# A timetable of a streaming block: the scores' pieces of blocks 2, 3 and of blocks 6, 7 are given earlier ticks

## What is computed

```
h   = RMSNorm(x)
[q|k|v|xc|B|C] = h @ W_in                          # 1024 x 3072
sb  = StickBreaking(QKNorm(q), QKNorm(k), v)       # 8 heads x 64, strictly causal
cv  = B * causal_depthwise_conv3(C * xc)           # 512 channels
x   = x + concat(RMSNorm(sb), RMSNorm(cv)) @ W_out
h2  = RMSNorm(x)
q1, q2 = halves of (h2 @ peer_w_q) per head (8 heads, 2 x 128)
s1, s2 = q1 @ sub_keys[0].T, q2 @ sub_keys[1].T    # 128 scores each
idx, gate = top 16 of the sums of top 16 of s1 and top 16 of s2; softmax
y   = x + sum over 8 heads, 16 picks of gate * gelu(h2 . U[idx]) * V[idx]
```

## Time and profile before

| | before |
|---|---|
| median of 3 runs | 2874.86 us (2873.90 to 2875.57) |
| profiled execution | 2879.8 us, span 2878.0 us |
| TensorE (PE) busy | 2225.2 us, 77% |
| VectorE (DVE) busy | 1983.9 us, 69% |
| ScalarE (ACT) busy | 1093.7 us, 38% |
| GpSimd (POOL) busy | 1103.9 us, 38% |
| DMA | 1183.89 MB, mean 411 GB/s |
| of it the gathers (q0) | 147456 packets, 1073.81 MB, 90.5% of 16 engines' span |
| weights, x and out (q1) | 108.17 MB, 9.6% |

### The profile page before, as it was taken

The page is one execution under the profiler, slowest core; times in us unless marked ns, Lnnn a source line. Parts: engine busy times, 40 slices in busy tenths (PEclk is TensorE's granted clock), DMA queues, the critical chain, the costliest instruction groups (busy, mean ns, idle before and its releaser), DMA issues. The chain is left out here.

```text
span 2878.0 us, 29917 instructions
## 1 busy us (share of the span) xinstructions
PE 2225.2 (77%) x9210; PEld 1012.2 (35%) x9210; DVE 1983.9 (69%) x4782; ACT 1093.7 (38%) x3164; POOL 1103.9 (38%) x1037
## 2 busy tenths in 40 slices
PE   9788889778977887778986888777898656555555
PEld 6535525333532343333542244333354111111111
DVE  3757766787666668786767666888666666666654
ACT  2333432552333335562333334666233322322222
POOL 0333433343343334443344333444334444434442
PEclk9999999989998998899998999999999776777787
DMA  9999999999999999999999999999999999999998
GB/s 390 359 413 403 398 419 418 419 412 412 385 421 420 419 419 412 419 415 416 412 420 420 418 410 416 410 417 415 419 405 420 416 422 419 421 418 416 415 421 353
DMA packets 178865, 1183.89 MB, mean 411 GB/s; under 512 B 19856, under 2 KB 21520, under 8 KB 47632
## 3 DMA queue, kind: packets, MB, share of 16 engines
q0 software_dynamic: 147456, 1073.81, 90.5%
q1 hardware_dynamic: 31248, 108.17, 9.6%
HBM read 1177.70 MB, written 4.19 MB: 411 GB/s over the span
## 5 line engine op out<-in xcount | busy, mean ns | idle before, releaser
L1472 DVE CUSTOM_DVE_ANT_0 ring<-ring,h2r 128x1024 f32<-128x1024 f32 x1024 | 1249.0, 1223 | 781.2 <-DMA ring<-table_uv,idx_t 772.1
L643 POOL DMA_INDIRECT ring<-table_uv,idx_t x1024 | 1102.0, 1076 | 1755.0 <-DVE dots L1472 1128.9
L911 PE MATMUL acc<-ring,wmask 128*64 128x512 f32 x4096 | 1200.6, 715 | 578.2 <-ACT wmask L1069 574.2
L911 PEld LDWEIGHTS acc<-ring,wmask 128*64 128x64 f32 x4096 | 283.4, 153 | 1286.4 <-ACT wmask L1069 845.9
L1064 ACT ACTIVATE dots<-dots 128x2 f32<-128x2 f32 x512 | 104.1, 203 | 1530.5 <-DVE dots L1472 1528.0
L1069 ACT ACTIVATE wmask<-gmask,dots 128x64 f32<-128x64 f32 x1024 | 300.3, 340 | 48.6 <-ACT dots L1064 1.5
L1057 ACT ACTIVATE gmask<-stack,gate_t 128x64 f32<-128x64 f32 x1024 | 293.1, 334 | 0.6 <-DVE gate_t L1459 0.5
L666 PE MATMUL pt<-hT,w_held 128*128 128x256 f32 (+1 forms) x560 | 109.3, 344 | 0.0
L666 PEld LDWEIGHTS pt<-hT,w_held 128*128 128x128 f32 x560 | 88.2, 193 | 28.2 <-issue 21.1
L1064 ACT ACT_TABLE_LOAD x73 | 93.7, 1283 | 1.3
L657 PE MATMUL pz<-w_ring,hT 128*128 128x512 f32 x192 | 90.8, 615 | 0.0
(11 more groups left out here) (274 smaller groups left out, 2171.6 us busy)
## 6 DMA issues: line engine op xcount, KB each, us to landing
w_ring<-wstream SPq DMA_DIRECT2D x121, 512.0 KB
ring<-wstream SPq DMA_DIRECT2D x32, 512.0 KB, 11.7
ring<-table_uv,idx_t POOLq DMA_INDIRECT x1024
w_held<-wstream SPq DMA_DIRECT2D x11, 512.0 KB, 13.4
xs<-x_in_dram SPq DMA_DIRECT2D x8, 512.0 KB
h2r<-wstream SPq DMA_DIRECT2D x8, 512.0 KB, 14.8
scores<-wstream SPq DMA_DIRECT2D x8, 512.0 KB, 15.4
xs<-wstream SPq DMA_DIRECT2D x4, 512.0 KB, 12.3
```

What stands on the lines that cost most here:

```text
L643: nc.gpsimd.indirect_dma_start(out=ring[:, cell(t):cell(t) + 2, :].rearrange("p c d -> p (c d)"), out_offset=None, in_=table, in_offset=ba ...
L911: mm = nc.tensor.matmul(acc[HALF * i:HALF * i + HALF, half * 512:(half + 1) * 512], wmask[:, slot, :], ring[:, cell(2 * p + i) + 1, half * ...
L1472: V.tensor_tensor_reduce(u, u, h2r[:, b % H_SLOTS, i, :], 1.0, 0.0, ALU.mult, ALU.add, dots[:, t % SLOTS:t % SLOTS + 1]).then_inc(dots_don ...
```

## The change

Two numbers of `WHEN` change: the middle tick of blocks 2 and 3 from 224 to 217, that of blocks 6 and 7 from 732 to 727. Start and end ticks stay.

```
 REST_BEGIN = 3
-WHEN = [(-1, -1, 16), (8, 66, 84), (72, 224, 262), (262, 470, 514), (521, 732, 775)]
+WHEN = [(-1, -1, 16), (8, 66, 84), (72, 217, 262), (262, 470, 514), (521, 727, 775)]
 RANK_TIME = [0, 2, 4, 7, 9, 11, 14, 15, 17, 20, 25]
```

## The result

| | before | after |
|---|---|---|
| median | 2874.86 us | 2883.30 us |
| lowest to highest of 7 runs each | 2872.92 to 2878.27 | 2880.47 to 2886.05 |
| profiled execution | 2879.8 us (span 2878.0) | 2883.3 us (span 2881.5) |

The ratio is 1.0025, with a 95% interval of 1.0015 to 1.0036, so 4.3 to 10.3 us more. A second series of the same two kernels, beside the experiments, gave 1.0017 (1.0008 to 1.0026). I had forecast 2871.9 us, with a range that ended at 2878.5.

The account below looks back on a forecast made before the run. The DMA gathers were taken as the bound, so a new order could only win or lose time short of gathers. Terms -3.5 + 0 + 0.5 + 0 = -3.0 us gave 2871.9 us, range 2865.5 to 2878.5.

Parts of the forecast that it names:

- Term (1): Blocks 2 and 3: scores six ticks ahead of the rank remove VectorE's 9.5 us wait; -3.5 us, bounds 0 and -6.4.
- Both estimates behind the 3.5: For the rank's wait: gather at 757.47 us delayed by 3.2 us; hole differences to other blocks, 3.5 and 4.9 us.
- rival A: At block 2's rank: TensorE's mixes held the gathers anyway, 0.5 us won and lost again; 2874.9 us, chance 0.15.
- Term (2): TensorE's rush in both block pairs moves seven and five ticks sooner, same contents, not eased; 0, bounds 5.8 won, 2 lost.
- Term (3): Steps before the middle ticks, 5% and 2.3% closer among the sticks; 0.5 us lost, bounds 1 won, 5.7 lost.
- The sign that I had set for trouble: Over either stretch of sticks, a rate under 410 GB/s would show the forecast wrong; 412 to 415 was expected.
- Term (4): 65 pick steps of blocks 1, 4 and 5 move by -3 to +4 ticks; 0, half a microsecond either way.
- Rival C: Closer sticks saturate VectorE, 9.1 us more lost there; slower by 5.6 us, up to 2882.5 us; chance 0.08.
- Rival B: Both holes at TensorE's rush close, backlog from late dots or full clock; 9.3 us won, 2865.6 us; chance 0.17.
- what I worked out beside it from the Trainium skill's page: Denser steps release the clock throttle, so blocks 2 and 3's rush starts at full clock; -5.8 instead of -3.0 us.

## Why the prediction was wrong, point by point

**Term (1), -3.5 us for the rank's wait: the first step that failed.** The wait went, as foretold, and was worth 0 (-2.3 to +2.6). Both estimates behind the 3.5 were unsound. The issue of one gather 3.2 us late was a true delay, though its row names a mix as releaser, and it went with the wait (1.24 us behind the one ahead, for 4.4), but the whole stretch from gather 216 to 230 is only 0.3 us shorter; a delay counts only if the gathers around it don't take it up. And 6.4 - 2.9 us compared one trace's hole with another place's, when the same program gave a hole of 4.5 us in place of 6.3 (ticks 208 to 230) in another execution. On this term rival A, at 0.15, was right; its time, 2874.9, was not.

**Term (2), the rush "with the same contents": the step that set the sign.** Its own pieces and mixes are the same. But I looked at what moves and not at what it moves past. `turn_picks(1,3)` keeps tick 215 and the look-ups beside it stay at 206 to 211; before, they stood ahead of the rush (214) or at its start, now they stand in it, from 207, and beside the root and the product of `h2`. The mean over ticks 208 to 230 is 7.2 us in the three traces with the changed program (9.5, 6.4, 5.7) and 4.9 in the three without it (6.3, 4.5, 3.8). The two groups overlap, and the kernel that is only pressed, with its rush where it was, lost 8.1; so the 2.3 us are a guess at the size. In ticks 716 to 745 the mean is 4.4 for the four that have blocks 6 and 7 changed (5.6, 3.7, 3.5, 4.8) and 2.7 for the three that don't (2.8, 2.4, 2.8). What ties the loss to these pick steps is the kernel with the quarters sooner: 4.8 and 2.4 us with the same rush, and a time that is level with before (0.9992).

**Term (3), 0.5 us for the closer steps.** For the sticks it holds as far as one can see: after has 406 GB/s from 1770 to 2010 us and its second trace 409, but of the kernels unchanged there one has 412 and another 407 over 240 us of the same work, against 414 in the earlier trace rows. The sign that I had set for trouble, under 410 GB/s, came in both, and tells little, since an unchanged kernel has it too. What the term left out is the end of the attention, where `sb_turn` and `root2` moved in between the look-ups of (1,2): ticks 185 to 193 lose 3.1 us in five traces with the changed order (2.1, 3.8, 3.8, 1.6, 4.0), 0.95 in the four without it (1.2, 0.3, 1.5, 0.8). Counted from tick 177 the difference is 1.7 us and the groups overlap. I took VectorE's load as an average over the stretch, 87%, and what was lost was lost in a few ticks.

**Term (4), 0 for the pick steps: the same mistake in other words.** I checked that `turn_picks` comes in time for its gather. I didn't check what VectorE and TensorE do in the tick where it stands. Both kinds mattered: `turn_picks(1,3)` kept its tick, and `look_up(1,2)` and `turn_picks(1,2)` are among the 65 that the planner moved, to just where TensorE then stood for 3.7 us. So the 2.1 us of ticks 185 to 193 belong to this term as much as to (3), against the half microsecond that I allowed it.

The three places make 2.1 + 2.3 + 1.7 = 6.1 us, inside the measured 4.3 to 10.3. The sizes come from three to five traces each that spread by 1 to 4 us, so the agreement may be luck; what stands is that the change costs, and that the moved quarters take the cost away.

**Rival C** gave the right side, for a wrong reason: VectorE's average load did not fill up. **Rival B**, and what I worked out beside it from the Trainium skill's page: the rush did not begin at the full clock. In after the granted clock is 0.57 from 704 to 712 us and TensorE, in order of time, has

```profile
704.83 3.68 PE L911 MATMUL acc<-ring,wmask 128*64 128x512 f32 x8 [2.94 <-ACT wmask L1069]
708.44 4.92 PE L666 MATMUL pt<-hT,vals_sb 128*128 128x256 f32 x16
```

again a mix of 3.68 us and a slow first piece, behind 2.94 us of idle time, as in the earlier trace rows. The rule of the Trainium skill ("TensorE: Matmul & The Clock Gate", Part 1: The HAM clock gate), that activity releases the throttle, agrees with the row. What failed is that denser steps would keep TensorE busy: it was idle until ScalarE's mask, behind dots that came late (none began between 696.80 and 702.64 us, with the root and its wait in between). In the kernel with the four quarters sooner the clock is 1.00 over ticks 208 to 230, against 0.95 and 0.98 in the change's two traces; this goes with the cure, and how much of the 4.7 us between 9.5 and 4.8 it makes was not separated. The clock alone does not set the loss: it was 0.96 over these ticks in the kernel with only blocks 6, 7 changed, which lost 4.5 us.

What stays open: how the rest of the sixteen stick passes of blocks 6 and 7 come to lose 1 to 7 us in ticks 600 to 620 from kernel to kernel, the unchanged ones among them (1.4 and 5.8 us); and how much of the rush's meeting is that the look-ups stand in it, how much `turn_picks`, and how much the root of `h2`. The kernel with `turn_picks` early lost 6.2 us there and the one with the last quarters sooner, where a look-up still meets the root, 4.3, which points at the look-ups in the rush; but that is one trace each.

## What to carry to other kernels

In a hand-made timetable a shift is not described by what moves but by the pairs that it brings together: list, for each engine, the steps that the shifted ones now pass or stand on, with the waits in them, and the steps that a planner moves in answer. Before a wait is priced, ask which other release the same consumer was waiting for; if that one comes no earlier, the wait is worth nothing, however long it is. And take a hole's depth from several executions, or from kernels that share the program at that place, before a difference of 3 us is put down to a cause.

## What the runs showed that I had not expected

- A wait of 8.6 to 9.5 us of the engine that feeds the bottleneck cost nothing measurable, twice: at the rank (ratio 1.0000) and at `turn_picks` (1.0028 without the wait, 1.0017 and 1.0025 with it). Steps of 0.7 to 2.6 us that met, with waits of 2 to 4 us in them, go with some 2 us lost at each of three places.
- Moving the middle tick earlier by 7 and 5, by 14 and 10, or later by 4 all made the kernel slower, by 0.17 to 0.37%. Yet the change at its full size costs nothing once four quarters of pick steps are moved too.
- The same program in ticks 208 to 230 lost 4.5 and 6.3 us in two traces, and 5.7, 6.4 and 9.5 in three of the changed one; ticks 8 to 72, the same in every kernel, lost between 3.3 and 8.2 us.
